# A four-layer attention trunk on one core: the second query block of the sliding-window layer, projected row tile by row tile

## The reference

```
def swa_sink_mixer(h, w_in, sinks, qn, kn):        # h = rms_norm(x), 256 x 1024
    proj = h @ w_in                                # 1024 -> 1024 (q) + 128 (k) + 128 (v)
    q = rope(rms_norm(proj[..., :D].reshape(B, S, 16, 64), qn))
    k = rope(rms_norm(proj[..., D:D + kvd].reshape(B, S, 2, 64), kn))
    v = proj[..., D + kvd:].reshape(B, S, 2, 64)
    s = q . k * 64 ** -0.5                         # each query sees its own and the previous chunk of 64
    pr = softmax([s, sink])[..., :-1]              # one sink logit per head
    return pr @ v
x = x + o @ w_o[i]
x = x + conv_ffn(rms_norm(x), ...)                 # gated MLP 1024 -> 2816 -> 1024 with a width-3 convolution
x = x + sigmoid(rms_norm(x) @ w_ple_gate[i]) * (p[i] @ w_ple_proj[i])
```

## Time and profile before

| | |
|---|---|
| Median of 3 runs | 1336.33 us (1332.82, 1336.33, 1336.37) |
| Profiled execution | 1334.3 us, its span 1332.5 us |
| Busy in the span | PE 1299.4 us (98%), DVE 1016.1 (76%), ACT 875.9 (66%), POOL 464.3 (35%) |
| Chain that ended last, by engine | PE 83%, DVE 8%, ACT 4%, POOL 2%, issue 2% |
| Mean granted TensorE clock | 0.992 |

### The profile page before, as it was taken

How to read it: one execution, slowest core, us unless ns; L and a number is a source line. 1 busy time by engine, 2 the same in 40 slices (tenths; PEclk the granted TensorE clock), 3 DMA queues, 4 the chain that set the end, 5 groups by cost and what they waited for, 6 DMA issues and landing times.

```text
span 1332.5 us, 22081 instructions
## 1 busy us (share of the span) xinstructions
PE 1299.4 (98%) x6932; PEld 1094.4 (82%) x6932; DVE 1016.1 (76%) x1615; ACT 875.9 (66%) x1569; POOL 464.3 (35%) x523
## 2 busy tenths in 40 slices
PE   6999999999999999999998899999999999999998
PEld 5888888888888888888876688888888888888886
DVE  5777898855777788885587888887476778888745
ACT  6776777744567677774465867776366777777533
POOL 3641245410275125550037315552014520455300
PEclk9999999999999999999997899999999999999999
DMA  7633555565674455656551265556456435555651
GB/s 259 227 112 111 190 190 188 187 213 170 200 231 138 143 181 186 191 188 209 165 175 64 96 198 184 189 188 219 158 183 204 129 125 174 186 187 189 211 175 63
DMA packets 64314, 232.39 MB, mean 174 GB/s; under 512 B 7440, under 2 KB 7568, under 8 KB 64240
## 3 DMA queue, kind: packets, MB, share of 16 engines
q1 hardware_dynamic: 61344, 221.35, 50.9%
q0 software_dynamic: 2896, 10.08, 2.4%
HBM read 230.35 MB, written 1.05 MB: 174 GB/s over the span
## 4 chain that ended last, share of the span: by engine, by line
PE 83%; DVE 8%; ACT 4%; POOL 2%; issue 2%; DMA 1%; POOLq 0%; DVEq 0%; SPq 0%; ACTq 0%
PE bank L1660 25%; PE bank L1413 24%; PE bank L1663 12%; PE bank L1389 5%; PE bank L1391 4%; PE bank L1390 4%; PE bank L1428 4%; DVE w_lo L800 4%; PE bank L1557 1%; PE bank L1580 1%; DMA w_raw<-weights 1%; ACT w_hi L457 1%; PE bank L1399 1%; DVE tok L844 1%; ACT hT L499 1%
## 5 line engine op out<-in xcount | busy, mean ns | idle before, releaser
L800 DVE TENSOR_TENSOR w_lo<-w_raw,w_hi 128x1024 fp32r<-128x1024 f32 x418 | 544.4, 1320 | 106.8 <-ACT w_hi L457 105.4
L457 ACT ACTIVATE w_hi<-w_raw 128x1024 fp32r<-128x1024 f32 x418 | 430.5, 1053 | 138.0 <-PE bank L1413 102.9
L1660 PE MATMUL bank<-hT,w_hi 128*128 128x512 f32 x1408 | 445.0, 396 | 2.1 <-DVE hT L859 2.1
L1663 PEld LDWEIGHTS bank<-hT,w_lo 128*128 128x128 f32 x1408 | 264.6, 188 | 59.7
L1663 PE MATMUL bank<-hT,w_lo 128*128 128x256 f32 x1408 | 282.0, 278 | 0.0
L1377 POOL TENSOR_TENSOR gT_lo<-gate_c,gT_hi 128x256 f32 (+1 forms) x88 | 170.8, 1941 | 201.4 <-ACT gT_hi L752 201.4
L1660 PEld LDWEIGHTS bank<-hT,w_hi 128*128 128x128 f32 x1408 | 216.6, 189 | 6.7 <-issue 3.7
L1389 PE MATMUL bank<-w_hi,hT 128*128 128x512 f32 (+1 forms) x336 | 134.2, 399 | 3.8 <-DVE hT L854 2.4
L1234 POOL TENSOR_TENSOR ssq<-ssq 128x1 f32<-128x1 f32 x24 | 7.9, 329 | 371.0 <-ACT tok L483 371.0
L1391 PE MATMUL bank<-w_hi,hT 128*128 128x512 f32 (+1 forms) x336 | 130.2, 387 | 0.0
L1390 PE MATMUL bank<-w_lo,hT 128*128 128x512 f32 (+1 forms) x336 | 130.0, 387 | 0.0
(11 more groups left out here) (162 smaller groups left out, 1998.5 us busy)
## 6 DMA issues: line engine op xcount, KB each, us to landing
w_raw<-weights SPq DMA_DIRECT2D x418, 512.0 KB, 3.5
gain<-gains POOLq DMA_DIRECT2D x11, 512.0 KB, 4.4
rel<-rel_in POOLq DMA_DIRECT2D x8, 256.0 KB, 3.7
x<-x_in SPq DMA_DIRECT2D x2, 512.0 KB, 5.3
out<-x SPq DMA_DIRECT2D x4, 256.0 KB, 2.0
p_end<-p_in POOLq DMA_DIRECT2D x3, 256.0 KB, 4.8
consts<-consts_in POOLq DMA_DIRECT2D x1, 392.0 KB, 3.5
conv_sb<-conv POOLq DMA_DIRECT2D x1, 352.0 KB, 4.2
```

The lines of the kernel that those rows point to most:

```text
L457: nc.scalar.activation(w_hi[:, slot, q * HALF:(q + 1) * HALF], w_raw[:, raw, :], ACT.Copy).then_inc(hi_ready, 1)
L800: nc.vector.tensor_tensor(w_lo[:, slot, cols], w_raw[:, half(q)[0], :], w_hi[:, slot, cols].bitcast(F32), ALU.subtract).then_inc(lo_ready, 1)
L1660: nc.tensor.matmul(up_banks(L, slot)[:, side, :], w_hi[:, *at(side)], hT[:, c, :, :], start=c == 0, stop=c == KC - 1, skip_group_check=True)
L1663: last = nc.tensor.matmul(up_banks(L, slot)[:, side, 0:SEQ], w_lo[:, *at(side)], hT_hi[:, c, :], start=False, stop=c == KC - 1, skip_group ...
```

## The change

Block 2's four pieces are taken in another order. Before, it is by half of the weight, both row tiles each: (g 0, t 0), (g 0, t 1), (g 1, t 0), (g 1, t 1). After, it is by row tile: (g 0, t 0), (g 1, t 0), (g 0, t 1), (g 1, t 1). Item 4 is so complete after the second piece and not after the third. Item 4 is copied out by ScalarE between the two halves of a weight split, and summed and turned by VectorE ahead of the steps. VectorE's place at the end of step 0, where item 4 was summed and turned, is taken by item 5; the place at the end of step 1, where item 5 was, is empty. Item 4 is transposed, copied and its rest taken in step 1 and not in step 2. GpSimd's list is unchanged, and item 5 is still copied out by ScalarE at the end of step 0 and turned by GpSimd in step 1.

```diff
-STEP_ITEMS = {FOX: {1: (6, 7)}, REL: {1: (6, 7)}, SWA: {2: (4,), 3: (5,)}}
+STEP_ITEMS = {FOX: {1: (6, 7)}, REL: {1: (6, 7)}, SWA: {1: (4,), 3: (5,)}}
...
 def pieces(m):
 
+    if m == SWA:
+        return [(2, g, t) for t in range(TT) for g in range(2)]
     return [(i, g, t) for i in range(2, len(BLOCKS[m])) for g in range(BLOCKS[m][i][2]) for t in range(TT)]
...
                 if m == SWA:
                     evacuate_item(3)
                     copy_items(0, 1)
-                    split_next(first + 1)
+                    split_half(first, 2)
+                    evacuate_item(4)
+                    split_half(first, 3)
                     copy_items(2)
                 else:
                     split_next(first + 1)
                 if m == SWA:
                     copy_items(3)
-                    evacuate_item(4)
...
                     sum_item(3)
                     turn_item(3)
                     rest_items(0, 1)
+                    sum_item(4)
+                    turn_item(4)
                     split_next(first + 1)
                     rest_items(2, 3)
...
-                    if m == SWA and s < 2:
-                        sum_item(4 + s)
-                        turn_item(4 + s)
+                    if m == SWA and s == 0:
+                        sum_item(5)
+                        turn_item(5)
...
-                    u = FIRST_IN[L] + len(pair_units) + j // 2
+                    u = FIRST_IN[L] + len(pair_units) + (g if m == SWA else j // 2)
```

## The result

The changed kernel takes 1339.90 us (median of 11 runs, 1337.63 to 1343.46) and the kernel before 1334.87 us (11 runs timed with it, 1332.82 to 1336.65). The ratio is 1.0040, 95% interval 1.0033 to 1.0048: 5.0 us slower. The forecast was slower, at 1341.0 us in a range of 1337.0 to 1344.0.

What follows compares the result with a forecast made beforehand. In layer 2's attention, waits through VectorE, ScalarE and GpSimd bound it until about 755 us, elsewhere TensorE. +4.56 (pair 1's inversion) + 0.6 (clock) = +5.2 us: 1339.5 from the profile, 1341.5 from the median; predicted 1341.0, range 1337.0 to 1344.0.

Steps and rivals of the forecast that it cites:

- Item 4's squares: ScalarE ahead of step 0: ready at 709.30 us, with VectorE idle 2.03 us until 709.35.
- First scores: TensorE in layer 2: `score_pair(0)` starts at about 714.45 us and not 711.30, 3.15 us later.
- My bound from below: Lower bound of the sum, 4.1 us: splits at their shortest, 0.4 us less, and no clock loss.
- Item 5's squares: ScalarE, step 0: end at 720.76 us, 3.28 us behind the sink's exponential; VectorE idle from 717.4 to 720.8.
- Pair 0's inversion: VectorE, end of step 0: at 724.97 us and not 718.87, 6.10 us late.
- What comes back: Between the inversions of pairs 0 and 1: 1.0 us from item 4's rest, 0.54 us from GpSimd's products.
- No slack up to the values of pair 5: Behind pair 1's inversion, 4.56 us late, the chain to 755 us takes up none of the delay.
- The clock: TensorE's fourth piece: a fall in the 3.0 us gap costs 0 to 1.1 us, taken as 0.6.
- the gain: Rival, chance 0.04: no waits for items 4 and 5, 1.27 and 1.0 us saved, 2.3 us faster, 1332.0 us.
- Clock falls and stays down: Rival: fourth piece and first scores at 1.2 GHz, GpSimd's part not regained, +6.2 us; chance 0.20 together with a collision.
- partly absorbed: Rival, chance 0.21: first 3.15 us real, item 5's wait costs little more or later steps absorb part; +2 to +3.9 us.
- The collision of the moved splits with GpSimd's turn of item 4: VectorE's splits waiting 1.31 us for `rope_c` on shared ports would make the sum +6.5 us; not counted on.

Runs made afterwards that it cites:

- gap-filled kernel: Changed kernel plus ten unused matmuls on TensorE ahead of layer 2's first scores; median 1337.65 us, ratio 1.0024 to the kernel before.
- item 5's sum late: Changed kernel with VectorE's sum and turn of item 5 back at the end of step 1; ratio 1.0021 to the kernel before, 1.0018 the second time.
- three comparisons: The changed kernel, unedited, timed three times beside the kernel before; ratios 1.0040, 1.0028 and 1.0028.
- both waits gone: Changed kernel with item 4's copy, sum and turn behind items 2 and 3, item 5's sum in step 1, item 4's transposes in step 2; ratio 1.0002.
- the third run: The changed kernel a third time, unedited, against the kernel before; median 1338.46 us, ratio 1.0028.
- item 4 behind: Changed kernel with item 4's copy, sum and turn behind the copies and rests of items 2 and 3; ratio 1.0028 to the kernel before.
- the two with both moved: Changed kernel with item 4's copy, sum and turn behind items 2 and 3, item 5's sum in step 1; ratio 1.0014, or 1.0002 with item 4's transposes in step 2.
- item 5 turned early: Kernel before with GpSimd's turn of item 5 in step 0, not step 1, without a wait for pair 2's sink sums; ratio 0.9998.

## Why the prediction was right

The mechanism was as forecast: two waits of VectorE for squares on ScalarE, and behind each the work that TensorE needs next. What each is worth by itself was not: taken away one after another, item 5's place and item 4 in step 1 account for nearly all of the stretch's loss, and the first wait for 0.1 to 0.3 us. Step by step, in time from the start of the stretch:

- *Item 4's squares*: forecast at 709.30, that is [7.67]. Measured 710.80 + 0.59, [7.66]. VectorE idle 2.03 forecast, 1.94 measured.
- *First scores*: forecast 3.15 us late, measured [12.31] against [9.67], 2.64 us. The step that was mis-sized is the split. I took the two halves at the 2.72 us that they cost before beside GpSimd's powers. They cost 714.97 - 712.69 = 2.28 us. Before, the first half took 1.67 us, begun while GpSimd's L1312 (128x512, 706.61 to 707.90) was at work, and the second 1.21 us; after, they took 1.22 and 1.21 us, though GpSimd's second power ran beside the first. So what had slowed the first half was most likely the end of item 3's turn, and not the powers. My bound from below had this 0.4 us, the value I took did not. It is 0.44 of the 0.51 us that the first scores came too early for the forecast.
- *Item 5's squares*: 3.28 us behind the sink's exponential forecast, 722.26 - 718.97 = 3.29 measured. VectorE idle 3.4 forecast, 3.36 measured.
- *Pair 0's inversion*: forecast 6.10 us late, measured [22.39] against [17.06], 5.33. Of the 0.77 us too much, 0.51 come from the first scores, the rest from small distances.
- *What comes back*: forecast 5.86 - 4.32 = 1.54 us. Measured [26.63] - [22.39] = 4.24 against 5.86: 1.62 us. GpSimd's products took 1.63 us and not 2.16.
- *No slack up to the values of pair 5*: pair 1 is inverted 26.63 - 22.92 = 3.71 us late, the stretch ends 3.73 us late. Right.
- *The clock*: forecast 0.6 of at most 1.08 us. In the profile that the sum is held against it cost nothing. It fell in the fourth piece in one of three profiles of this kernel and cost 0.3 to 0.5 us there, which over the three is 0.1 to 0.2 us. Whether 0.6 was too much for the median is open. Three profiles do not give the share of executions, the gap-filled kernel's median was 1.0 us lower, and a fall in the gap itself costs more: with item 5's sum late, item 5's squares then ended at [20.21] and not at [18.53].

In the stretch there are +3.7 us where I had 4.56, and with the clock as the three profiles have it +3.9 where I had 5.2. Side by side the medians differ by 5.0, 4.2 and 3.4 us in three comparisons (the third 1338.46 against 1335.08). The last two fit what the stretch shows. That the first is a microsecond above it stays open. Its longest runs are those with the lowest mean granted clock: 1337.63 us at 0.993, 1340.97 and 1343.46 us at 0.988. But only the profiled execution shows where it fell, and the clock also falls at 691 us, which has nothing to do with the change.

So the predicted 1341.0 was 1.1 us high. I measured from the median of the three runs, 1336.33, which is 1.5 us above the median of the eleven; my sum was 0.2 us over the first difference of the medians; and I took 1341.0 where the sum gave 1341.5, without a reason. That the 5.2 us of the sum came so near the 5.0 us of the first comparison is luck: the sum was 1.5 us over the stretch, and that comparison lies 1.3 us over the stretch for a reason that stays open. Over the other two it was 1.0 and 1.8 us. The forecast's own range was also written wrongly: +4.1 to +5.9 on the median's basis is 1340.4 to 1342.2 us, and not 1339.5 to 1342.5.

Of the rivals, *the gain* was not only absent, it was mispriced. I gave it 2.3 us, 1.27 of them from ahead of pair 1's masks. With both waits gone, nothing is gained (53.62 against 53.38, the collision included), and moving item 4 to step 1 costs 1.3 us (54.89 against 53.62). The main reason is in the rows: before the change item 4's sum ran in time in which pair 1's scores were being made anyway. They start at [13.51], the mask of pair 0 followed its scores by 1.10 us, and the mask of pair 1 began at 716.59, [14.96]; so only 0.35 us could be had. *Clock falls and stays down* has the clock's part shown in the third run, at 0.3 to 0.5 us where it had 1.08; GpSimd's 0.54 us were regained. By its size the stretch's 3.7 us falls into the span of *partly absorbed* (2 to 3.9 us), but not by its mechanism: pair 1 was inverted 3.71 us late and the stretch ended 3.73 us late, so nothing was taken up behind it. One part of the wait for item 5 did cost nothing, though. With the sum late the masks of pair 1 began at [17.14], behind their scores, and in the changed kernel at [19.83]: 2.7 us, out of 3.36 us of waiting and 1.27 us of sum and turn.

The collision of the moved splits with GpSimd's turn of item 4, which I did not count, cost VectorE nothing, but not for the reason I gave: `rope_c` began at 714.26, before the splits ended at 715.04, and it was `rope_c` that took longer, 1.92 us and not 1.31. The sink sums of pairs 0 and 1 took 0.16 us each in the changed kernel. In four of the experiments such sums collided (item 4 behind, the two with both moved, and item 5 turned early). The Trainium skill (SBUF — State Buffer, section "SBUF: two separate sides") says that the loser of the shared ports stands still for the whole instruction. The traces agree: 1.13 us, until GpSimd's instruction ended near 716.4, and 1.19 and 1.12 us against 0.16 with GpSimd out of the way.

## What to carry to other kernels

Work put ahead of its old place on an in-order engine is not free when its input is younger than what is queued behind it: look up when the input is ready, and add the idle time to everything behind it. When one item's work moves forward and the next item's work moves into the freed slot, check the second one's producer too; here its place was worth 1.7 to 2.1 of 3.7 us. A gap that a trace shows is not a price: item 4's was 2.64 us wide at the first scores and worth 0.1 to 0.3 us at the end, since other waits lay behind it. Before pricing a gain, ask when the thing behind the removed work could have started on its own.

## What the runs showed of the hardware

VectorE's instructions on 128x4 values, 0.16 us each, took up to 1.20 us beside GpSimd's additions and products of 128x512 (1.18 us at 713.83; 1.19 and 1.12 us in the ungated version). A wait that kept GpSimd off them, 0.72 us long, gave 0.9 us of the stretch back (51.49 to 50.62).

TensorE's granted clock is not the same from one execution to the next over the same instructions: behind a gap of 2.56 to 2.59 us it stayed at 1.00 in three profiles (stretches of 57.11, 56.91 and 55.02 us) and fell in two (57.40 and 57.45). What a fall cost: 0.3 to 0.5 us in the changed kernel, where nine of the piece's matmuls were slow (the first of them in part) and VectorE waited for item 5's squares anyway; 2.4 us with item 5's sum late, where the first ten were slow and VectorE waited for the scores behind them.
